# Smaller transfers of x, a later mean and an fp32 column-group projection in a two-layer encoder trunk

## The reference

```python
for l in range(DEPTH):
    h = h + hybrid_mixer(rmsnorm(h, norm1_g[l]), w_in[l], b_f[l], ...)
    h = h + conv_glu_ffn(rmsnorm(h, norm2_g[l]), w_up[l], ...)
return rmsnorm(h, final_g)
# rmsnorm(x, g) = x * rsqrt(mean(x * x) + eps) * g
# hybrid_mixer: u = xn @ w_in gives qa, ka, va, qb, kb, vb, qc, kc, vc and fc (4 columns, one a head)
# log_f = log_sigmoid(fc + b_f); its cumulative sum over the frames biases the attention of branch C
```

## Time and profile before

| | us |
|---|---|
| median of 3 runs (1487.49 to 1489.11) | 1487.55 |
| the profiled execution | 1488.57 |
| its span in the trace | 1486.6 |

### The profile page before, as it was taken

The page is one execution under the profiler, slowest core; times in us unless marked ns, Lnnn a source line. Parts: engine busy times, 40 slices in busy tenths (PEclk is TensorE's granted clock), DMA queues, the critical chain, the costliest instruction groups (busy, mean ns, idle before and its releaser), DMA issues.

```text
span 1486.6 us, 19540 instructions
## 1 busy us (share of the span) xinstructions
PE 1473.5 (99%) x7022; PEld 1215.9 (82%) x7022; DVE 975.7 (66%) x1614; ACT 665.9 (45%) x1140; POOL 45.1 (3%) x35
## 2 busy tenths in 40 slices
PE   8999999999999999999999999999999999999998
PEld 6888888888888888888878888888888888888886
DVE  7777666565687734776477876665647776357753
ACT  6655555444444422443475555544345443234434
POOL 0000000002100000000200000000030000000001
PEclk9999999999999999999999999999999999999999
DMA  6222222232332233332432222222333332333331
GB/s 231 88 83 71 85 71 73 71 93 78 128 99 91 83 99 110 99 93 71 134 116 89 66 86 78 65 78 80 98 103 95 99 95 82 101 105 98 99 105 66
DMA packets 42560, 139.61 MB, mean 94 GB/s; under 512 B 5364, under 2 KB 5492, under 8 KB 42232
## 3 DMA queue, kind: packets, MB, share of 16 engines
q1 hardware_dynamic: 41760, 137.13, 29.3%
q10 hardware_dynamic: 728, 1.52, 0.3%
HBM read 136.53 MB, written 2.10 MB: 93 GB/s over the span
## 4 chain that ended last, share of the span: by engine, by line
PE 96%; ACT 1%; DVE 1%; DMA 1%; issue 1%; ACTq 0%; SPq 0%; DVEq 0%
PE dense L630 28%; PE dense L632 28%; PE dense L631 28%; PE turned L695 2%; PE branch L722 1%; PE dense L875 1%; PE dense L874 1%; PE dense L873 1%; DMA h<-in_x 1%; PE scores L683 1%; PE scores L682 1%; PE branch L708 1%; PE scores L686 0%; ACT tmp L1093 0%; ACT whi L943 0%
## 5 line engine op out<-in xcount | busy, mean ns | idle before, releaser
L630 PE MATMUL dense<-hg,whi 128*128 128x512 f32 x1376 | 547.7, 398 | 3.0 <-DVE hg L1285 2.6
L632 PE MATMUL dense<-hg,wlo 128*128 128x512 f32 x1376 | 537.4, 391 | 0.0
L631 PE MATMUL dense<-hg,whi 128*128 128x512 f32 x1376 | 537.0, 390 | 0.0
L943 ACT ACTIVATE whi<-raw 128x1024 fp32r<-128x1024 f32 (+3 forms) x269 | 265.4, 987 | 439.1 <-PE dense L632 417.5
L1272 DVE TENSOR_TENSOR wlo<-raw,whi 128x1024 fp32r<-128x1024 f32 (+3 forms) x269 | 305.9, 1137 | 180.2 <-ACT whi L943 177.9
L630 PEld LDWEIGHTS dense<-hg,whi 128*128 128x128 f32 x1376 | 259.6, 189 | 58.3 <-issue 4.8
L632 PEld LDWEIGHTS dense<-hg,wlo 128*128 128x128 f32 x1376 | 258.8, 188 | 55.0
L631 PEld LDWEIGHTS dense<-hg,whi 128*128 128x128 f32 x1376 | 259.4, 189 | 51.7 <-issue 1.0
L630 PE MATMUL dense<-act,whi 128*128 128x512 f32 x528 | 207.2, 393 | 0.0
L632 PE MATMUL dense<-act,wlo 128*128 128x512 f32 x528 | 205.6, 389 | 0.0
L631 PE MATMUL dense<-act,whi 128*128 128x512 f32 x528 | 205.5, 389 | 0.0
(11 more groups left out here) (188 smaller groups left out, 1269.8 us busy)
## 6 DMA issues: line engine op xcount, KB each, us to landing
raw<-in_w_up SPq DMA_DIRECT2D x88, 512.0 KB, 3.5
raw<-in_w_gate SPq DMA_DIRECT2D x48, 512.0 KB, 3.5
raw<-in_w_in SPq DMA_DIRECT2D x35, 512.0 KB, 3.5
raw<-in_w_down SPq DMA_DIRECT2D x32, 384.0 KB, 3.0
raw<-in_w_out SPq DMA_DIRECT2D x16, 512.0 KB, 3.4
raw<-in_w_down SPq DMA_DIRECT2D x16, 320.0 KB, 2.9
raw<-in_w_down_last SPq DMA_DIRECT2D x10, 512.0 KB, 3.5
raw<-in_w_br_a SPq DMA_DIRECT2D x8, 512.0 KB, 3.4
```

The lines of the kernel that those rows point to most:

```text
L630: mm(out, a, xhi, start=start, stop=False)
L631: mm(out, a, xlo, start=False, stop=False)
L632: return mm(out, b, xhi, start=False, stop=stop)
L943: fn(whi[:, s, 0:cols], raw[:, r, 0:cols], ACT.Copy).then_inc(w_hi.sem, 1)
```

## The change

1. x comes in eight transfers of one chunk: ACT's queue issues chunks 0 and 2 with the gains and half of tile 0, later 5 and 7; SP's queue issues 1, 3, 4 and 6 behind the first half of tile 0, without the waits that stood between them.
2. In layer 0 the mean stands inside unit 2, after its fifth chunk, no longer after unit 1.
3. The forgetting weights are multiplied by the gains on DVE into `wf_g` (32 columns a chunk, 28 of them zero). PE multiplies them with `h` itself in plain fp32: 8 products, chunk c into rows 32 * (c % 4) onward of `bank_t`. DVE scales all 128 rows by `rt` in one operation, and a further fp32 product with a 0/1 matrix `fold` (ahead of the next unit) adds the four groups. The splits of `wf` on ACT and DVE are gone.

```diff
-            def load_x(c):
-                sp.dma_start(h[:, 2 * c:2 * c + 2, :], A["x"][:, 2 * c:2 * c + 2, :]).then_inc(x_in_s[c], 16)
-
-            load_x(0)
-            sp.wait_ge(half_in, 16)
-            load_x(2)
-            sp.wait_ge(x_in_s[0], 16)
+            for c in (1, 3, 4, 6):
+                sp.dma_start(h[:, c, :], A["x"][:, c, :]).then_inc(x_in_s[c], 16)
...
@@ PE, ahead(l, n)
                 if n == F_AT[l]:
-                    pe.wait_ge(wf_lo_s.sem, wf_lo_s.at(l, 0))
+                    pe.wait_ge(wf_s.sem, wf_s.at(l, 0))
                     pe.wait_ge(rms.sem, rms.at(l, 0))
+                    pe.wait_ge(h_new.sem, h_new.at(l, -1))
                     for c in range(C):
-
-                        if c > 0:
-                            mm(bank_t[0:4, :], wf_hi[:, c, :], hg[:, 1, c, :], start=False, stop=False)
-                        last = mm(bank_t[0:36, :], wf_st[:, c, :], hg[:, 0, c, :], start=c == 0, stop=c == C - 1)
-                        if c == 0:
-                            mm(bank_t[0:4, :], wf_hi[:, c, :], hg[:, 1, c, :], start=False, stop=False)
+                        r = slice(32 * (c % 4), 32 * (c % 4) + 32)
+                        last = mm(bank_t[r, :], wf_g[:, c, :], h[:, c, :], start=c < 4, stop=c >= 4)
                     last.then_inc(f_ps.sem, 1)
+                if n == F_AT[l] + 1:
+                    pe.wait_ge(f_x.sem, f_x.at(l, 0))
+                    mm(bank_t[0:4, :], fold, f_lin[:, :], start=True, stop=True).then_inc(f_ps.sem, 1)
@@ PE, mixer_unit(l, n), after each chunk i
+                    if (l, n, i) == (0, 2, C // 2):
+                        pe.wait_ge(const_in, 16)
+                        mean_squares(l, 0)
@@ DVE, loop over n
-                    if n == 0:
-                        dve.wait_ge(wf_hi_s.sem, wf_hi_s.at(l, 0))
-                        ve.tensor_tensor(wf_lo, wf[:, :, :], wf_hi.bitcast(F32), ALU.subtract).then_inc(wf_lo_s.sem, 1)
...
                     if n == 0:
                         continue
+                    if n == F_AT[l] - 1:
+                        dve.wait_ge(wf_in, 16 * l + 16)
+                        dve.wait_ge(wf_zero, 3)
+                        row = gains[:, 2 * l * C:2 * l * C + C]
+                        ve.tensor_tensor(wf_g[:, :, 0:4], wf[:, :, :], row.unsqueeze(2).to_broadcast([P, C, 4]),
+                                         ALU.mult).then_inc(wf_s.sem, 1)
                     if l > 0 and n == 1:
                         scale_tables(l)
@@ DVE, forget_x(l)
-                ve.tensor_tensor(f_aux[0:4, :], bank_t[32:36, :], rt[32:36, :], ALU.mult).then_inc(f_x.sem, 1)
-                ve.tensor_tensor(f_lin[0:4, :], bank_t[0:4, :], rt[0:4, :], ALU.mult).then_inc(f_x.sem, 1)
-                dve.wait_ge(f_x.sem, f_x.at(l, 1))
-                ve.tensor_tensor(f_lin[0:4, :], f_lin[0:4, :], f_aux[0:4, :], ALU.add).then_inc(f_x.sem, 1)
+                ve.tensor_tensor(f_lin[:, :], bank_t[:, :], rt[:, :], ALU.mult).then_inc(f_x.sem, 1)
```

More of the change, by code:

```diff
@@ L47 @@
 LOWEST = -3e38
-WARM = 16
+WARM = 17
 RAW = 4
@@ L154, in const_array @@
     parts["own_rows"] = np.arange(P)[:, None] // 32 == np.arange(4)[None, :]
+    parts["fold"] = np.arange(P)[:, None] % 32 == np.arange(4)[None, :]
     parts["own_half"] = np.arange(P)[:, None] // HD == np.arange(2)[None, :]
@@ L161 @@
 for _name, _n in (("ident", P), ("mean", P), ("mask_b", P), ("mask_c", S),
-                  ("spread1", 2), ("own_rows", 4), ("own_half", 2), ("eps", 1)):
+                  ("spread1", 2), ("own_rows", 4), ("fold", 4), ("own_half", 2), ("eps", 1)):
     CONST_AT[_name] = (CONST_COLS, _n)
@@ L282, in build @@
         spread1, own_rows, own_half, eps = const("spread1"), const("own_rows"), const("own_half"), const("eps")
+        fold = const("fold")
         gains = sb("gains", [P, 2 * L * C])
@@ L287, in build @@
         wf = sb("wf", [P, C, 4])
-        wf_st = sb("wf_st", [P, C, 36], F32R)
-        wf_hi, wf_lo = wf_st[:, :, 0:4], wf_st[:, :, 32:36]
+        wf_g = sb("wf_g", [P, C, 32])
+        blank = sb("blank", [P, 2 * P], F32R)
         stat = sb("stat", [P, 2, T])
@@ L362, in build @@
         const_in = sem("const_in")
-        x_in_s = [sem(f"x_in{i}") for i in range(C // 2)]
+        x_in_s = [sem(f"x_in{i}") for i in range(C)]
         tab_in = sem("tab_in")
@@ L380, in build @@
         rt_done = signal("rt_done", 2)
-        f_ps = signal("f_ps", 1)
-        f_x = signal("f_x", 3)
+        f_ps = signal("f_ps", 2)
+        f_x = signal("f_x", 1)
         f_abs = signal("f_abs", 1)
@@ L587, in _ @@
                         load_mixer(l, n)
-                    if l == 0 and n == 1:
-                        sp.wait_ge(x_in_s[2], 16)
                     if l == 0 and n == 2:
@@ L910, in _ @@
             pe.wait_ge(wf_zero, 2)
-            zeros = wf_st[:, :, :].rearrange("p c n -> p (c n)")
             for _ in range(WARM):
-                mm(bank_t[0:36, 0:2 * P], zeros[:, 0:36], zeros[:, 0:2 * P], start=True, stop=True)
+                mm(bank_t[0:32, 0:2 * P], blank[:, 0:32], blank[:, :], start=True, stop=True)
             for l in range(L):
@@ L973, in root, with load_x @@
                 fn(rt[:, :], bank_t[:, :], ACT.Sqrt, bias=eps).then_inc(rms.sem, 1)
+            def load_x(c):
+                act.dma_start(h[:, c, :], A["x"][:, c, :]).then_inc(x_in_s[c], 16)
+            load_x(0)
             act.dma_start(gains[:, :], A["gains"]).then_inc(gains_in, 16)
+            load_x(2)
             act.dma_start(raw[:, 0, SLOT // 2:SLOT], A["w_in"][0, 0, :, SLOT // 2:SLOT]).then_inc(raw_in[0], 16)
-            act.dma_start(h[:, 2:4, :], A["x"][:, 2:4, :]).then_inc(x_in_s[1], 16)
             act.wait_ge(warm, 1)
@@ L995, in _ @@
                 first_hi(c)
-                if c == 0:
-                    act.dma_start(h[:, 6:8, :], A["x"][:, 6:8, :]).then_inc(x_in_s[3], 16)
-                if c == 1:
+                if c < 2:
+                    load_x(5 + 2 * c)
+                if c == 3:
                     act.wait_ge(raw_in[0], 16)
@@ L1005, in forget_abs @@
                 act.wait_ge(small_in, 16 * l + 16)
-                act.wait_ge(f_x.sem, f_x.at(l, 2))
-                fn(f_aux[0:4, :], f_lin[0:4, :], ACT.Abs, bias=small[0:4, 3 * C + 8:3 * C + 9]).then_inc(f_abs.sem, 1)
+                act.wait_ge(f_ps.sem, f_ps.at(l, 1))
+                fn(f_aux[0:4, :], bank_t[0:4, :], ACT.Abs, bias=small[0:4, 3 * C + 8:3 * C + 9]).then_inc(f_abs.sem, 1)
             def forget_exp(l):
@@ L1180, in _ @@
                         fn(stat[:, 1, 0:1], eps, ACT.Sqrt)
-                    if n == 0:
-                        act.wait_ge(wf_in, 16 * l + 16)
-                        act.wait_ge(wf_zero, 2)
-                        fn(wf_hi, wf[:, :, :], ACT.Copy).then_inc(wf_hi_s.sem, 1)
                     if n == MEAN_AT[l]:
@@ L1324, in forget_sum @@
                 dve.wait_ge(small_in, 16 * l + 16)
-                ve.tensor_scalar(f_min[0:4, :], f_lin[0:4, :], small[0:4, 3 * C + 8:3 * C + 9], 0.0,
+                ve.tensor_scalar(f_min[0:4, :], bank_t[0:4, :], small[0:4, 3 * C + 8:3 * C + 9], 0.0,
                                  ALU.add, ALU.min).then_inc(f_mn.sem, 1)
@@ L1725, in add_square @@
                     nc.gpsimd.tensor_tensor(ssum[:, :], ssum[:, :], sq[m % 2][:, :], ALU.add).then_inc(ssum_done.sem, 1)
-            zeros = k[:, 4, 0:C * 36]
+            zeros = k[:, 4, 0:2 * P]
             nc.gpsimd.memset(zeros, 0.0).then_inc(wf_zero, 1)
             pool.wait_ge(wf_zero, 1)
-            nc.gpsimd.tensor_copy(wf_st[:, :, :].rearrange("p c n -> p (c n)"), zeros).then_inc(wf_zero, 1)
+            nc.gpsimd.tensor_copy(blank[:, :], zeros).then_inc(wf_zero, 1)
+            nc.gpsimd.memset(wf_g[:, :, :].rearrange("p c n -> p (c n)"), 0.0).then_inc(wf_zero, 1)
             pool.wait_ge(late_in, 32)
```

24 lines of the change are left out of this document (9 added, 15 removed).

## The result

The changed kernel takes 1496.56 us (median of 5 runs, 1495.88 to 1497.04). Beside it the kernel before took 1488.09 (5 runs, 1487.49 to 1489.11). The ratio is 1.0056, with a 95% interval of 1.0044 to 1.0068: 8.5 us slower. The forecast was 1496.8. The time is thus what was said, but two of the steps that lead to it were not, and that their errors cancelled is luck; the experiments take them apart. The profiled execution of the changed kernel took 1495.88 us, with a span of 1494.1.

The account below looks back on a forecast made before the run. The prediction took PE, busy 99% of the span, as the bound. Layer 0's +3.9 and layer 1's +2.7 make +6.6: 1488.57 + 6.6 + 2.6 (clock) - 1.02 (profile to median) = 1496.8 us, range 1490.5 to 1500.5.

Parts of the forecast that it names:

- Part 3, the new wait: Ahead of the projection PE waits for DVE's `wf_g`: 5.9 us in layer 0, +1.4 us in layer 1.
- The clock: Behind layer 0's gap of 5.9 us PE falls to 1.2 GHz, costing +2.6 us; nothing in layer 1.
- Part 2, the mean: Inside layer 0's unit 2 at T + 3.41, taking 0.87 us; the 1.25 us wait for the sum of squares goes.
- Part 1, T: At the start: tile 1 lands at 12.6, unit 1 begins at 15.1, unit 2 at 20.6 (18.9 to 21.3), before 22.2.
- those chunks are done when tile 1 lands: At the start: the last two x chunks are finished by tile 1's landing, leaving 2.5 us of copy and subtraction before unit 1.
- Part 4, P: The projection's 8 fp32 products take 3.9 us; with the fold, less the former 3.72, +1.3 us a layer.
- a P below 3: Sign of a wrong prediction: the projection's products taking under 3 us, where 3.9 was forecast.
- two run at a time whatever the number of groups: In the projection, record order lets only two fp32 records run at once: 3.49 us for 512 columns, plus burst costs.
- the 2.0 as a bound: Lower bound of the projection's time: all four groups at once, two rounds of 0.87 us; the upper bound was 7.2.
- rival C: In the projection four column groups run at once: 3.8 us less, 1493.0 with the fallen clock, 1490.4 without; chance 0.17.
- The fold: Behind unit 3, one fp32 product of one group, 0.87 + 0.25 = 1.1 us; its operand is done 5 us earlier.

Follow-up runs that it names:

- the product early: The changed kernel with `wf_g` made on DVE at tile 1 of a layer, ahead of the reciprocal and rotary work; 1488.42 us.
- filling the gap: The changed kernel with 42 unread products of zeros ahead of PE's wait for `wf_g` in layer 0; 1494.12 us.
- the mean alone: The kernel before with only the mean's place in layer 0 moved inside unit 2; 1488.72 us beside 1488.25.
- the loads alone: The kernel before with only the change's eight one-chunk transfers of x; 1489.52 us beside 1488.20.
- all parts: The mended start with the mean behind the third chunk of unit 2, and the fold and what follows one unit later; 1487.12 us.
- mended start: The product early, plus x1, x3, x5, x6, x7 on SP's queue ahead of tile 1, x4 up front on ACT's, 38 warm-up products, not 17; 1486.35 us.
- x first: The changed kernel with every load of x issued ahead of tile 1 and the constants; 1495.39 us.
- all three kernels: The mended start (1486.35 us), all parts (1487.12 us), and the mended start with only the mean moved behind unit 2's third chunk (1485.38 us).

## Why the prediction came out right, and where it was wrong

- **Part 3, the new wait: right**, and it is what makes the kernel slower. `wf_g` was said to keep PE idle for 5.9 us, with the projection at T + 12.2; it was 5.62 and T + 12.1 (T, the start of unit 2, being 23.19). Layer 1: +1.4 said, +1.36 measured (764.71 - 757.01 against 756.37 - 750.03). With the product early all of it goes.
- **The clock: right in what happens**, 2.6 us said, 2.1 to 2.4 measured by filling the gap. But the row that gave the 2.6 was misread. The 5.26 us at half speed at the start were taken for what a gap of 2.35 leaves behind, and the products ahead of that gap had run no faster:

```profile
1.62 3.63 PE L913 MATMUL turned<-wf_st 128*36 128x256 f32 x16 [1.62 <-POOL wf_st L1730]
```

Sixteen products of 256 columns, 0.21 us apart, where the last of the longer warm-up come every 0.11. The clock had not risen yet, so it had not fallen. That the size is near is luck.
- **Part 2, the mean: right as a time** (T + 3.40 against T + 3.41, no wait). That the place is worth nothing by itself wasn't said; the mean alone shows it.
- **Part 1, T: wrong.** Said was 20.6, measured 23.19. The step that failed is "those chunks are done when tile 1 lands". Tile 1 landed at 10.8, 1.8 us earlier than I took, but x7 landed at 14.16, and unit 1 waits for both. I had asked which bytes come in front of tile 1 and not which come in front of the last x. T lies outside its own range of 18.9 to 21.3. Against the kernel before, the loads were to bring 1.6 us and cost 0.9 in the profile, 1.3 in the medians of the loads alone.
- **Part 4, P: wrong**, and it is the mis-sized term. P was 3.9 and is 1.98 at 2.4 GHz; a P below 3 was one of the prediction's own signs of being wrong. The step that failed is "two run at a time whatever the number of groups"; four do. I had the 2.0 as a bound and as rival C and set them aside for an argument about the order of records, where the nearest rows fitted both. The fold was right (1.1 said, 1.07 measured). P + F - 3.72, with 0.10 that the projection now begins late, is -0.57 a layer instead of +1.3, 3.7 us less in all.

In layer 0 the projection takes 3.9 us (from 35.32 to the second product behind it, at 39.49, less one product), the very number forecast, but for another reason: four at once, at half the clock. A reader who looked at layer 0 alone would have taken the step as shown.

The sum, profile against profile: said were -1.6 for the loads, +8.1 to unit 4 and its clock (30.7 against 22.58), +2.7 in layer 1, together 9.2. Measured were +0.9, +5.7 and +0.7, together 7.3. The loads were 2.5 too low; the rest was 4.4 too high. That 1.9 us too much became 0.2 has a third reason: I took off 1.02 us from the profiled time to the median, while the five runs of the kernel after lie 0.7 above its profile. By mechanism the case that came true is rival C's packing with the fallen clock (1493.0), with a T 2.6 us later than it was given.

One loss of the new projection stood in no sum. Between unit 4 and the mean of layer 1 the kernels with it (all parts apart) take 0.3 to 0.8 us more than the kernel before (711.1 to 711.5 against 710.74). Lined up product by product, 0.13 us of it lie in the first products behind the fold and 0.25 ahead of the first scores near 58 us. The latter is the forget gate's later chain: with the early product DVE's last operation ahead of the scores ends at 58.59, when PE has been free since 58.57, and in the kernel before it ends at 58.22, ahead of PE at 58.45. The kernels with the mended start lose another 0.24 at 327 us; why stays open.

## What to carry to other kernels

When an operation is made anew, look where its engine's queue puts it: 0.18 us of work behind a long dependent chain cost 8.1 us here, the fall of the clock included, and cost nothing ahead of it. A wait that goes gains nothing while another engine's chain, started by the same result, sets the next unit; follow that chain before crediting the wait. And of loads in order of use, the last one that anything needs counts: give it a place in the queue, and the queue a share of the wires, ahead of what is needed later.

## What the runs showed of the chip that I had not expected

- Products of fp32 on four groups of 32 columns run four records at once, 0.43 us for each four at 2.4 GHz and 0.85 at 1.2, in both orders of the groups that were run. Two groups run two.
- Two full queues sent the same number of rows in the same three us, 201 and 202, though those of one were longer: 770 KB for rows of 3.6 to 4 KB, 412 KB for rows of 2 KB.
- Waits of 1.02, 1.19, 1.56 and 1.66 us in a busy stretch left the granted clock at 1.00. One of 5.62 did not: it fell in the wait, at 32.93. At the start, all or nearly all of the 16 or 17 warm-up products ran at half speed. Behind them the kernel after began unit 0 at 0.23 us a product and fell to 0.43 at 9 us; the kernel before, the filled gap and x first ran at 0.43 from the first product on. With 38 warm-up products all three kernels ran at 0.23 from the first.
